# The norms between the stages of a two-block transformer pair: which instructions stand in their chain, and TensorE products repeated in their wait

## The chip, the cores and the metric

One Trainium2 chip, one of its cores. The time is device microseconds of one execution; lower is better. TensorE is called PE, VectorE DVE, ScalarE ACT, GpSimd POOL and SyncE SP.

## The reference

x is 256 tokens of 1024 values in float32. It goes through two blocks of a first kind, and then through two blocks of a second kind. A block of the first kind ends both of its halves with a layer norm of the residual, one of the second kind begins both of its halves with an rms norm:

```python
for l in range(DEPTH):                      # first kind, DEPTH = 2
    y = hybrid_mixer(x, ...)
    x = layer_norm(DN_ALPHA * x + y, ln1_g[l], ln1_b[l])
    y = conv_gated_ffn(x, ...)
    x = layer_norm(DN_ALPHA * x + y, ln2_g[l], ln2_b[l])
...
y = rmsnorm(x, g)                           # second kind: norm_mix, and norm_ffn alike
    # = x * rsqrt(mean(x * x) + NORM_EPS) * g
x = x + branch(y)
```

## The kernel before, in words

Everything runs as one long stream of weight products. A weight is cut into "halves" of 128 x 1024 values, 602 in all. Each half is loaded into `raw`, copied by ACT to a rounded high part `hi` (line 344), and POOL subtracts the two to get the low part `lo` (line 353). PE then makes three products for each tile (lines 146 to 148: high by high, low by high, high by low). There are four buffers of halves (`HALVES`), so the copy of half h waits for the products of half h - 4. `Stream.act`, `.pool`, `.dve` and `.pe` issue this stream on each engine up to a position; `end()` of a stage is 2 x (its last half + 1). `main.act(act, self.end())` therefore includes the copy of the fourth half of the next stage, which waits for the very last product of this one.

Between two stages stands a norm, where PE has nothing to multiply. The 256 tokens are two tiles of 128 tokens (tt = 0, 1), each in two column halves of 512. The last weight of a stage gives its sums in this order: tile 0 columns 0 to 511, tile 0 the rest, tile 1 the same, some 0.7 us apart. `Stream.by_tokens` changes that for the last four halves of the program: first all their products for tile 0, then all for tile 1.

- `Norm1` (`ln1` and `ln2` of the first kind, four times): DVE adds the residual (line 1046), takes statistics (1048, 1050), ACT takes the root (1022), DVE the reciprocal (1054) and writes `xn` (1057). PE transposes `xn` in 16 pieces (1011), ACT applies gain and bias (1029), DVE splits the result into `x_hi` (1075) and `x_lo` (1077), pair by pair of the eight 128-row pieces, and PE starts on the next stage's products as the pairs come. POOL rebuilds the residual `x_tok` from `xn` (lines 1095 and 1096), a quarter in the wait and the others between the coming low parts.
- The last `Norm1` has no transposes. DVE alone makes its full result in `x_tok` (1057, 1065, 1066), and the first `Norm2` follows on that.
- `Norm2` (`norm_mix` and `norm_ffn`, four times): the same with DVE statistics (1182 to 1185), root 1156, reciprocal 1189, `xn` 1192, transposes 1145, `x_hi` on ACT 1163 and `x_lo` on DVE 1198.
- `Final`: squares and their sum on ACT (1230), in place of DVE statistics.

## Time and profile before

| | us |
|---|---|
| median of 3 runs | 2162.07 (2160.2 to 2164.91) |
| profiled execution, its own time | 2160.19 |
| its span | 2158.4 |
| PE busy | 2084.0 (97%) |
| ACT busy | 1059.7 (49%) |
| POOL busy | 1498.1 (69%) |
| mean granted clock of PE | 0.984 of full |

The table is read from the left: the span is what the profile covers, and the execution's own time is 1.8 us more. Busy times overlap. A granted clock of 1.0 is 2.4 GHz and 0.5 is 1.2 GHz.

### The profile page before, as it was taken

What the parts mean: (1) busy time and instruction counts of PE and PEld (TensorE: products, weight loads), DVE (VectorE), ACT (ScalarE), POOL (GpSimd) and SP (SyncE); (2) the same over time, 40 slices, a digit from 0 to 9 for tenths busy, and PEclk for the clock granted to TensorE, in tenths of its full rate; (3) what the DMA queues carried; (4) which work ended last, traced back from release to release, by engine and by line L of the source; (5) the groups of instructions that cost most, each with busy time, mean ns of one, the idle gap of its engine ahead of it and who ended that gap; (6) DMA issues with size and microseconds to landing.
All of it is one profiled execution on the core that took longest, in us unless ns stands there. A gap on an engine that the chain in (4) does not pass through costs nothing.

```text
span 2158.4 us, 38524 instructions
## 1 busy us (share of the span) xinstructions
PE 2084.0 (97%) x16616; PEld 1921.1 (89%) x16616; DVE 899.3 (42%) x1498; ACT 1059.7 (49%) x1500; POOL 1498.1 (69%) x632
## 2 busy tenths in 40 slices
PE   7989989999969999999999899999999999998998
PEld 6889978799959989899999899899898999998998
DVE  5353247465355547374113211355473651132112
ACT  5555554555546453256444444465532564444444
POOL 6679887689856535367778688765353677786886
PEclk9999999999989999999999999999999999999999
DMA  8436544435534323234445455533232444454553
GB/s 346 142 126 208 193 166 141 154 121 195 193 137 137 118 82 116 99 137 157 156 157 191 149 187 181 190 137 119 79 118 91 145 157 156 157 182 151 184 187 127
DMA packets 47193, 332.89 MB, mean 154 GB/s; under 512 B 5168, under 2 KB 5552, under 8 KB 7856
## 3 DMA queue, kind: packets, MB, share of 16 engines
q1 hardware_dynamic: 47024, 330.43, 44.2%
q8 instruction: 131, 2.15, 0.4%
q14 instruction: 38, 0.31, 0.0%
HBM read 329.36 MB, written 1.05 MB: 153 GB/s over the span
## 4 chain that ended last, share of the span: by engine, by line
PE 68%; DVE 2%; ACT 1%; issue 0%; POOL 0%; DVEq 0%; ACTq 0%
PE bank L146 16%; PE bank L147 15%; PE bank L148 15%; PE y L146 3%; PE y L148 3%; PE y L147 3%; PE bank L1816 1%; PE bank L1828 1%; PE bank L1826 1%; PE bank L1856 1%; PE bank L1873 1%; PE bank L1876 1%; PE bank L1657 1%; PE bank L1867 1%; DVE bn L1182 1%; PE bank L1757 0%
## 5 line engine op out<-in xcount | busy, mean ns | idle before, releaser
L353 POOL TENSOR_TENSOR w_lo<-w_raw,w_hi 128x1024 fp32r<-128x1024 f32 x602 | 1462.4, 2436 | 642.8 <-ACT w_hi L344 642.6
L344 ACT ACTIVATE w_hi<-w_raw 128x1024 fp32r<-128x1024 f32 x602 | 636.7, 1059 | 929.0 <-PE bank L148 759.3
L146 PE MATMUL bank<-x_hi,w_hi 128*128 128x256 f32 x2960 | 866.2, 293 | 18.0 <-POOL w_lo L353 13.3
L147 PE MATMUL bank<-x_lo,w_hi 128*128 128x256 f32 x2960 | 842.0, 284 | 0.0
L148 PE MATMUL bank<-x_hi,w_lo 128*128 128x256 f32 x2960 | 841.8, 284 | 0.0
L146 PEld LDWEIGHTS bank<-x_hi,w_hi 128*128 128x128 f32 x2960 | 572.0, 193 | 41.1 <-issue 19.1
L147 PEld LDWEIGHTS bank<-x_lo,w_hi 128*128 128x128 f32 x2960 | 572.7, 193 | 6.7 <-issue 4.8
L148 PEld LDWEIGHTS bank<-x_hi,w_lo 128*128 128x128 f32 x2960 | 572.0, 193 | 0.0
L881 DVE SCALAR_TENSOR_TENSOR conv<-bank,par_sb,conv 128x254 f32<-128x254 f32 (+1 forms) x176 | 76.8, 478 | 213.7 <-ACT conv L869 212.1
L1298 DVE TENSOR_TENSOR hid_lo<-hid,hid_hi 128x512 fp32r<-128x512 f32 x22 | 45.1, 2048 | 241.2 <-ACT hid_hi L1293 241.2
L146 PE MATMUL y<-w_hi,hid_hi 128*128 128x512 f32 x352 | 139.9, 397 | 3.7 <-DVE hid_lo L903 3.7
L148 PE MATMUL y<-w_hi,hid_lo 128*128 128x512 f32 x352 | 139.0, 395 | 0.0
L147 PE MATMUL y<-w_lo,hid_hi 128*128 128x512 f32 x352 | 139.0, 395 | 0.0
L146 PEld LDWEIGHTS y<-w_hi,hid_hi 128*128 128x128 f32 x352 | 66.3, 188 | 19.7 <-DVE hid_lo L903 5.8
L148 PEld LDWEIGHTS y<-w_hi,hid_lo 128*128 128x128 f32 x352 | 66.2, 188 | 15.8
L1436 DVE SCALAR_TENSOR_TENSOR conv<-bank,par_sb,conv 128x255 f32<-128x255 f32 (+1 forms) x144 | 62.5, 477 | 41.3 <-ACT conv L1427 39.6
L147 PEld LDWEIGHTS y<-w_lo,hid_hi 128*128 128x128 f32 x352 | 66.2, 188 | 13.8
L1560 DVE SCALAR_TENSOR_TENSOR gate<-gate,bank 128x512 f32<-128x512 f32 x16 | 11.0, 688 | 130.5 <-PE bank L148 130.5
L146 PE MATMUL bank<-w_hi,x_hi 128*128 128x512 f32 x128 | 53.3, 416 | 0.0
L147 PE MATMUL bank<-w_lo,x_hi 128*128 128x512 f32 x128 | 50.0, 391 | 0.0
L148 PE MATMUL bank<-w_hi,x_lo 128*128 128x512 f32 x128 | 50.0, 391 | 0.0
L869 ACT ACTIVATE conv<-bank,par_sb 128x256 f32<-128x256 f32 x88 | 44.1, 551 | 0.0
(394 smaller groups left out, 3003.2 us busy)
## 6 DMA issues: line engine op xcount, KB each, us to landing
w_raw<-w SPq DMA_DIRECT2D x300, 1024.0 KB, 4.8
ln_rows<-ln_rows SPq DMA_DIRECT2D x4, 1024.0 KB, 7.7
mem_tok<-mem SPq DMA_DIRECT2D x2, 1024.0 KB, 4.9
const_sb<-const SPq DMA_DIRECT2D x1, 1536.0 KB, 8.2
par_sb<-par SPq DMA_DIRECT2D x2, 553.5 KB, 10.8
xn<-xT SPq DMA_DIRECT2D x1, 1024.0 KB, 4.9
w_raw<-w SPq DMA_DIRECT2D x2, 512.0 KB, 5.0
x_tok<-x SPq DMA_DIRECT2D x1, 1024.0 KB, 6.9
```

The costliest lines, as they stand in the source:

```text
L146: pe.matmul(out, lhs[0], rhs[0], start=start, stop=False, skip_group_check=skip)
L147: pe.matmul(out, lhs[0], rhs[1], start=False, stop=False, skip_group_check=skip)
L148: return pe.matmul(out, lhs[1], rhs[0], start=False, stop=stop, skip_group_check=skip)
L344: act.activation(self.hi[:, h % HALVES, :], self.raw[:, n % RAWS, i * HW:(i + 1) * HW], ACT.Copy).then_inc(*sig.up("high", h))
L353: pool.tensor_tensor(self.lo[:, h % HALVES, :], self.raw[:, n % RAWS, i * HW:(i + 1) * HW], self.hi[:, h % HALVES, :].bitcast(F32), ALU.su ...
L869: ins = act.activation(cb[:, j, :], view[:, j, :], ACT.Identity, scale=taps[:, 2, c0 + j:c0 + j + 1], bias=bias[:, c0 + j:c0 + j + 1])
L881: ins = dve.scalar_tensor_tensor(cb[:, j, tap:T], view[:, j, 0:T - tap], taps[:, 2 - tap, c0 + j:c0 + j + 1], cb[:, j, tap:T], ALU.mult, A ...
L1182: ins = dve.bn_stats(net.bn[:, tt, half, :], net.xtok[:, tt, c])
L1298: dve.tensor_tensor(net.hs2[1][:, 2 * (i % 3):2 * (i % 3) + 2, :], m["hid"][:, i % 2, :, :], net.hs2[0][:, 2 * (i % 3):2 * (i % 3) + 2, :] ...
L1436: ins = dve.scalar_tensor_tensor(cb[:, j, tap:T], two(b)[:, j, 0:T - tap], taps[:, 3 - tap, c0 + j:c0 + j + 1], cb[:, j, tap:T], ALU.mult, ...
L1657: pe.matmul(bank[b][:, :], K("ones"), m["keys"][:, j, :, :].rearrange("p i t -> p (i t)"), start=True, stop=True).then_inc(*sig.up("key_su ...
L1816: mm = pe.matmul(yd[g][r, (n % 4) * CH:(n % 4 + 1) * CH], h["mt"][r, n, :], h["t"][r, n, :], start=True, stop=True)
```

## The change

It touches the seven places between stages, and nothing inside them:

1. **Norm1** (three places). ACT gets its root table before the last two weight copies, and the fourth copy of the next stage moves behind the norm. ACT writes `xn` of tile 0; DVE only that of tile 1. POOL's first rebuild of `x_tok` waits until all of `xn` is there. PE repeats 14 products of the old `x_hi` behind the stage's last one, and 7 more behind tile 0's transposes.
2. **Norm2** (three places). Table load and fourth copy move alike. ACT squares and sums `x_tok` in place of DVE's statistics, and writes the last quarter of `xn`. PE repeats 12 products.
3. **Border** (a new class; it replaces the last `Norm1` and the first `Norm2`). The last four halves of `w_down` are ordered by tokens, so that tile 0 is normalised during tile 1's products; for this the last three down units stand at the stage's end. A norm's four DVE passes of 128 x 512 over a tile take the place of six. Transposes and splits go by tile. PE repeats 52 products, and 10 small ones of the identity between the tiles.

```diff
-    def by_tokens(self, first):
-        group = range(first, first + HALVES)
-        self.parts[2 * first:2 * (first + HALVES)] = [(h, part) for part in range(2) for h in group]
+    def by_tokens(self, last):
+        first = last + 1 - HALVES
+        group = range(first, last + 1)
+        self.parts[2 * first:2 * (last + 1)] = [(h, part) for part in range(2) for h in group]
...
@@ Feed1.__init__
-            if i:
+            if 0 < i < (11 if l < DEPTH - 1 else 9):
                 self.units.append(self.add_down(i - 1))
-        self.units.append(self.add_down(10))
+        for i in ((10,) if l < DEPTH - 1 else (8, 9, 10)):
+            self.units.append(self.add_down(i))
...
@@ Norm1.pe
         net.main.pe(pe, self.end())
+        net.repeat(pe, self.tb[3], 14)
         for tt in range(TT):
+            if tt:
+                net.repeat(pe, net.bank[4], 7)
...
@@ Norm1.act
-        net.main.act(act, self.end())
+        net.main.act(act, self.end() - 6)
+        act.preload_act_table_set("sqrt_and_others")
+        net.main.act(act, self.end() - 2)
...
+            if tt == 0:
+                act.wait_ge(*sig.at("inverse", *k_l))
+                act.wait_ge(*sig.at("product", self.after().last))
+                for half in range(2):
+                    c = slice(half * HALF, (half + 1) * HALF)
+                    act.activation(net.xn[:, 0, c], net.xtok[:, 0, c], ACT.Identity, scale=net.rs[:, 0:1], bias=net.ms[:, 0:1]
+                                   ).then_inc(*sig.up("xn_act", *k_l, half))
...
+        net.main.act(act, self.end())
@@ Norm1.dve, the new order
+        residual(0, 0)
+        statistics(0, 0)
+        residual(0, 1)
+        statistics(0, 1)
+        variance(0)
+        residual(1, 0)
+        inverse(0)
+        dve.scalar_tensor_tensor(net.ms[:, 0:1], net.mv[:, 0, 0:1], -1.0, net.rs[:, 0:1], ALU.mult, ALU.mult
+                                 ).then_inc(*sig.up("inverse", *k_l))
+        statistics(1, 0)
+        residual(1, 1)
+        statistics(1, 1)
+        variance(1)
+        inverse(1)
...
@@ Norm1.pool
         net.main.pool(pool, self.end())
...
+        pool.wait_ge(*sig.at("xn_act", *k_l, 1))
+        pool.wait_ge(*sig.at("xn", *k_l, 1))
...
@@ Norm2.pe and Norm2.act
+        net.repeat(pe, self.tb[3], 12)
...
+            act.wait_ge(*sig.at("x_new", *k_l, tt, 1))
+            act.activation(net.xn2[:, tt, :], net.xtok[:, tt, :], ACT.Square, accum_out=net.ms[:, tt:tt + 1]
+                           ).then_inc(*sig.up("x_squared", *k_l, tt))
...
+        act.wait_ge(*sig.at("inverse", *k_l))
+        act.activation(net.xn2[:, 1, HALF:D], net.xtok[:, 1, HALF:D], ACT.Copy, scale=net.rs[:, 1:2]).then_inc(*sig.up("xn_act", *k_l))
...
@@ Border.pe
+        net.main.pe(pe, self.end())
+        net.repeat(pe, self.tb[0][3], 52)
+        for tt in range(TT):
+            if tt:
+                pe.wait_ge(*sig.at("var", *self.first, 1))
+                for _ in range(10):
+                    pe.matmul(self.tb[1][3][:, 0:P], net.K("ident"), net.K("ident"), start=True, stop=True)
...
@@ Border.act
+        main.act(act, self.end() - 6)
+        act.preload_act_table_set("sqrt_and_others")
+        root_first(0)
+        act.wait_ge(*sig.at("x_new", *self.second, 0, 0))
+        main.act(act, self.end() - 4)
+        squares(0)
+        root(0)
+        root_first(1)
...
+        main.act(act, self.end())
...
@@ Net
+    def repeat(self, pe, bank, times):
+        for _ in range(times):
+            pe.matmul(bank[:, 0:T], self.xs[0][:, 0, 0:P], self.xs[0][:, 0, :], start=True, stop=True)
```

Three places show what moves. In the names, `w_hi` is a weight copy, `sd` the root, `xn` and `xn_189` the normalised tokens and `x_sb`, `x_hi` the transposed ones; numbers behind a name are buffers.

ACT at `ln1` of the first block, before:

```order
L344 ACTIVATE w_hi<-w_raw 128x1024 x3
L1022 ACT_TABLE_LOAD
L1022 ACTIVATE sd_60<-mv,const_sb 128x1 x2
L1029 ACTIVATE x_sb<-bank,par_sb 128x256 x8
L344 ACTIVATE w_hi<-w_raw 128x1024 x2
```

and after:

```order
L1022 ACT_TABLE_LOAD
L345 ACTIVATE w_hi<-w_raw 128x1024 x2
L1027 ACTIVATE sd_60<-mv,const_sb 128x1
L1033 ACTIVATE xn<-x_tok,ms_59,rs_61 128x512 x2
L1027 ACTIVATE sd_60<-mv,const_sb 128x1
L1039 ACTIVATE x_sb<-bank,par_sb 128x256 x8
L345 ACTIVATE w_hi<-w_raw 128x1024 x3
```

The table load stands two copies earlier, one of the copies has gone behind the eight `x_sb` steps, and two `xn` steps are new between the roots.

ACT at the border, from the last `hid_hi` on, before:

```order
L861 ACTIVATE hid_hi<-hid 128x512
L344 ACTIVATE w_hi<-w_raw 128x1024 x4
L1022 ACT_TABLE_LOAD
L1022 ACTIVATE sd_60<-mv,const_sb 128x1 x2
L1156 ACTIVATE sd_60<-ms_59,const_sb 128x1 x2
L1163 ACTIVATE x_hi<-bank,par_sb 128x256 x8
L344 ACTIVATE w_hi<-w_raw 128x1024 x2
```

and after, where line 1265 is the layer norm's root, 1272 a square, 1277 the rms norm's root, 1299 `xn` and 1284 `x_hi`:

```order
L861 ACTIVATE hid_hi<-hid 128x512
L345 ACTIVATE w_hi<-w_raw 128x1024 x3
L1289 ACT_TABLE_LOAD
L1265 ACTIVATE sd_60<-mv,const_sb 128x1
L345 ACTIVATE w_hi<-w_raw 128x1024
L1272 ACTIVATE xn_189,bn<-x_tok 128x512 x2
L1277 ACTIVATE ms_59<-ms_59,const_sb 128x1
L1265 ACTIVATE sd_60<-mv,const_sb 128x1
L1299 ACTIVATE xn_189<-x_tok,rs_61 128x512 x2
L1284 ACTIVATE x_hi<-bank,par_sb 128x128 x4
L1272 ACTIVATE xn_189,bn<-x_tok 128x512 x2
L1277 ACTIVATE ms_59<-ms_59,const_sb 128x1
```

Three copies instead of four stand ahead of the load, a fourth ahead of the squares, and the squares and `xn` steps are ACT's now.

DVE at the border, before, from the last statistics of the layer norm on:

```order
L1048 BN_STATS bn<-x_tok 128x6
L1050 BN_AGGR mv<-bn 128x2
L1054 RECIPROCAL rs_61<-sd_60 128x1
L1057 TENSOR_SCALAR xn<-x_tok,mv,rs_61 128x512
L1065 TENSOR_TENSOR x_tok<-xn,ln_rows 128x512
L1066 TENSOR_TENSOR x_tok<-x_tok,ln_rows 128x512
L1057 TENSOR_SCALAR xn<-x_tok,mv,rs_61 128x512
L1065 TENSOR_TENSOR x_tok<-xn,ln_rows 128x512
L1066 TENSOR_TENSOR x_tok<-x_tok,ln_rows 128x512
L1054 RECIPROCAL rs_61<-sd_60 128x1
```

and after, from its first variance on (1336 subtracts the mean and multiplies by the gain, 1343 multiplies by the reciprocal and adds the bias):

```order
L1328 BN_AGGR mv<-bn 128x2
L1336 SCALAR_TENSOR_TENSOR x_tok<-x_tok,mv,ln_rows 128x512 x2
L1340 RECIPROCAL rs_61<-sd_60 128x1
L1343 SCALAR_TENSOR_TENSOR x_tok<-x_tok,rs_61,ln_rows 128x512 x2
L1323 SCALAR_TENSOR_TENSOR x_tok<-x_tok,y 128x512
L1325 BN_STATS bn<-x_tok 128x6
L1348 TENSOR_TENSOR ms_59<-bn 128x1
L1323 SCALAR_TENSOR_TENSOR x_tok<-x_tok,y 128x512
L1325 BN_STATS bn<-x_tok 128x6
L1328 BN_AGGR mv<-bn 128x2
L1353 RECIPROCAL rs_61<-ms_59 128x1
L1336 SCALAR_TENSOR_TENSOR x_tok<-x_tok,mv,ln_rows 128x512 x2
```

Tile 0's layer norm now stands ahead of tile 1's residual, and each tile's passes are four instead of six.

## Rows read from the trace of the kernel before

**Rows 1.** The page: span, PE busy and its granted clock in 40 slices
```profile
span 2158.4 us, 38524 instructions
...
PE   7989989999969999999999899999999999998998
...
PEclk9999999999989999999999999999999999999999
```

**Rows 2.** Waits of PE over the span: total us, times, longest us
```profile
PE bank L1145 <- DVE xn L1192: 30.9, 4, 16.0
PE bank L1011 <- DVE xn L1057: 14.6, 7, 4.5
PE bank L146 <- POOL w_lo L353: 13.3, 3, 11.4
```

**Rows 3.** Windows: stretch, its length, each engine's busy us and starts, granted clock, DMA
```profile
110.60:120.39 9.79, 4.05 (x19) 2.45 (x17) 9.09 (x17) 5.28 (x10) 6.36 (x4) 0.78 0.54 202
120.39:126.30 5.91, 5.91 (x28) 5.91 (x29) 2.94 (x6) 1.76 (x5) 0.00 (x0) 0.50 0.00 0
...
323.36:327.70 4.34, 4.34 (x20) 4.34 (x21) 2.94 (x6) 1.41 (x4) 0.00 (x0) 0.50 0.01 4
...
433.36:437.00 3.64, 3.64 (x17) 3.64 (x18) 2.94 (x6) 1.40 (x4) 0.00 (x0) 0.51 0.00 0
626.00:646.77 20.77, 3.71 (x19) 3.10 (x17) 17.90 (x39) 5.41 (x12) 4.20 (x2) 0.67 0.30 101
646.77:652.70 5.93, 5.93 (x48) 5.91 (x49) 2.54 (x8) 2.20 (x5) 1.45 (x1) 1.00 0.00 0
1196.15:1205.84 9.69, 4.02 (x18) 3.30 (x17) 7.40 (x19) 4.82 (x10) 3.58 (x2) 0.82 0.55 201
1205.84:1211.80 5.96, 5.96 (x49) 5.93 (x50) 2.21 (x6) 2.20 (x5) 1.48 (x1) 1.00 0.01 3
...
1962.51:1966.10 3.59, 3.59 (x17) 3.59 (x18) 2.20 (x6) 1.13 (x4) 0.00 (x0) 0.50 0.02 5
```

**Rows 4.** Timeline of DVE, norm ln1 of the first block: start, us, [idle before]
```profile
108.96 0.69 DVE L1046 SCALAR_TENSOR_TENSOR x_tok<-x_tok,y 128x512 f32<-128x512 f32 x1 [5.58 <-PE y L148]
...
114.85 1.00 DVE L1057 TENSOR_SCALAR xn<-x_tok,mv,rs 128x512 f32<-128x512 f32 x2
...
115.96 2.70 DVE L1057 TENSOR_SCALAR xn<-x_tok,mv,rs 128x512 f32<-128x512 f32 x2
...
119.55 0.69 DVE L1077 TENSOR_TENSOR x_lo<-x_sb,x_hi 128x512 fp32r<-128x512 f32 x1
```

**Rows 5.** Timeline of ACT and POOL in the same norm
```profile
112.17 1.28 ACT L1022 ACT_TABLE_LOAD   x1
...
115.54 1.43 POOL L1095 TENSOR_TENSOR x_tok<-xn,ln_rows 128x512 f32<-128x512 f32 x1 [0.96 <-DVE xn L1057]
```

**Rows 6.** Timeline of DVE and ACT, norm_ffn of the first block
```profile
1194.49 0.69 DVE L1180 TENSOR_TENSOR x_tok<-x_tok,y 128x512 f32<-128x512 f32 x1 [13.17 <-PE y L148]
...
1201.96 0.89 DVE L1192 TENSOR_SCALAR xn<-x_tok,rs 128x512 f32<-128x512 f32 x2
...
1203.95 2.67 ACT L1163 ACTIVATE x_hi<-bank,par_sb 128x256 fp32r<-128x256 f32 x7 [2.75 <-PE bank L1145]
```

**Rows 7.** Timeline of DVE and ACT in the last norm
```profile
2146.07 1.39 DVE L1249 TENSOR_TENSOR x_tok<-x_tok,y 128x512 f32<-128x512 f32 x2 [6.30 <-PE y L148]
...
2151.65 1.38 DVE L1249 TENSOR_TENSOR x_tok<-x_tok,y 128x512 f32<-128x512 f32 x2 [1.27 <-PE y L148]
...
2146.79 0.63 ACT L1230 ACTIVATE xn<-x_tok 128x512 f32<-128x512 f32 x1 [3.18 <-DVE x_tok L1249]
```

**Rows 8.** Timeline of POOL in the products behind ln1
```profile
139.74 1.62 POOL L1096 TENSOR_TENSOR x_tok<-x_tok,ln_rows 128x512 f32<-128x512 f32 x1
141.32 9.95 POOL L353 TENSOR_TENSOR w_lo<-w_raw,w_hi 128x1024 fp32r<-128x1024 f32 x4
```

**Rows 9.** One line of DVE: count, shortest/median/longest ns, first and last start
```profile
L1298 DVE TENSOR_TENSOR hid_lo<-hid,hid_hi x22: 1996/2006/2480, 1225.7 to 2137.3; 128x512 fp32r<-128x512 f32 x22
```

More of the change, by code:

```diff
@@ L922, in last_low @@
             state_low(dve, 10)
-        self.units[-3].dve = last_low
+        last.dve = last_low
     def add_down(self, i):
@@ L1105, in sp @@
                          ).then_inc(*sig.up("pos_loaded", by=16))
-        net.main.send(sp, net.main.halves[self.after().last][0] + 1 + (5 if self.last else 12 if self.key == "ln1" else 9))
+        net.main.send(sp, net.main.halves[self.after().last][0] + 1 + (12 if self.key == "ln1" else 9))
         if self.l == 0:
@@ L1126, with __init__ @@
 class Norm2:
[L1129 removed]
+    def __init__(self, net, key, l, after, more):
         self.net, self.key, self.l, self.after, self.more = net, key, l, after, more
@@ L1182, in dve @@
-                ins = dve.bn_stats(net.bn[:, tt, half, :], net.xtok[:, tt, c])
-            step(ins)
-            step(dve.bn_aggr(net.mv[:, tt, :], net.bn[:, tt, :, :]))
-            dve.scalar_tensor_tensor(net.ms[:, tt:tt + 1], net.mv[:, tt, 0:1], net.mv[:, tt, 0:1], net.mv[:, tt, 1:2],
-                                     ALU.mult, ALU.add).then_inc(*sig.up("var", *k_l, tt))
+                if tt == TT - 1 and half == 1:
+                    dve.wait_ge(*sig.at("product", self.after().last))
+                else:
+                    dve.wait_ge(*sig.at("summed", self.more, tt, half))
@@ L2048, in act @@
         self.weighted_high(act, 5)
-        main.act(act, 2 * (self.units[-1].last + 1))
+        main.act(act, 2 * (self.units[-1].last + 1) - 2 * HALVES)
     def chain_act(self, act, hf, key_log):
@@ L2482, in __init__ @@
         self.main = Stream(sig, raw, hi, lo, units)
-        self.main.by_tokens(len(self.main.halves) - HALVES)
+        for s in self.stages:
+            if isinstance(s, (Border, Final)):
+                self.main.by_tokens(s.after().last)
     def K(self, name):
```

260 lines of the change are left out of this document (183 added, 77 removed).

## The prediction

> **What bounds the kernel now.** I read the page first [rows 1]. PE is busy in nine tenths or more of nearly every slice, and its granted clock is full outside a few slices. So the products set the time, and only the places where PE has none can be shortened. The list of PE's waits names them [rows 2]: transposes behind `xn`, 30.9 us for four `Norm2` (16.0 of it at the border) and 14.6 us for three `Norm1`. The 13.3 us behind POOL are 11.4 us at the start of the program, which the change doesn't touch.
>
> The windows put a length on each place, from the start of a stage's last product to the first product of the next [rows 3]: 9.79 us at `Norm1` (three such places, alike within 0.04 us), 9.69 us at `Norm2` (three, alike within 0.01), 20.77 us at the border. They also show a second cost. The clock falls to 0.5 in each wait, and in four of seven places the next stage's products begin at it: for 5.91, 4.34, 3.64 and 3.59 us. At 0.5 half of such time is lost, 8.7 us in all. Behind the border and behind `norm_ffn` of the first block the clock was back at 1.00 when the products began.
>
> **Norm2, three places.** Before, the first residual starts at 1194.49, `xn` of tile 1 at 1201.96, `x_hi` at 1203.95 and the first product at 1205.84 [rows 3, 6]. After, DVE only adds: tile 0 is whole 1.4 us after 1194.49, at 1195.9, and tile 1's last half, which waits for the last product, at 1197.3. A square of 512 columns takes ACT 0.63 us [rows 7]; for 1024 I take 1.1, and 0.2 for reading the sum, 0.3 for the root. That gives tile 0's root at 1197.5 and tile 1's at 1199.0. Reciprocal and half an `xn` (0.89 / 2) end at 1199.6. The last quarter of `xn` is ACT's, beside it. Two transposes at the full clock and their latency bring `x_hi` to 1200.05 instead of 1203.95. Behind it nothing changes, so each place saves 3.9 us, **11.6 us** for three. The bounds: 3.0 if the square costs 0.4 more for each tile, 4.3 if the tiles overlap better. The 12 repeats cost nothing: 48 starts in 5.93 us are 0.12 us each [rows 3], 1.5 us behind a last product at 1196.4, and tile 0's `xn` isn't there before 1198.1.
>
> **Norm1, three places.** Here DVE keeps the statistics. Its tile 0 `xn` goes to ACT (1.00 us of DVE less [rows 4]), one reciprocal and a one-column product (0.4) go ahead of tile 1's statistics, and tile 1's root is no longer covered (0.4). So tile 1's `xn` starts at 115.7 instead of 115.96. What matters more is its length: before, both halves took 2.70 us beside POOL's `x_tok`, against 1.00 us for the pair ahead of it [rows 4, 5]. POOL now waits. The first half is ready 1.0 us earlier, and transposes at the full clock give 0.3: 1.3 us a place, **3.9 us**. The fillers (1.7 us, then 0.8) end before the `xn` they might hold up, at 112.7 against 113.6, and at 115.4 against 116.3.
>
> The Trainium skill (GPSIMD Engine Reference, Specifications) says that POOL shares its SBUF interfaces with DVE instructions of two SBUF inputs or in a two-port mode; by that rule the four passes of the border are exposed too, and the next part takes it up with a row.
>
> **The table load.** Its 1.28 us ends at 113.45 [rows 5], ahead of DVE's need for the first root, so its move is worth nothing by itself; it only makes the earlier reciprocal possible. The Trainium skill (ScalarE: Activation LUTs, What ACT_TABLE_LOAD costs) adds a drain and comes to 2.66 us for a switch: by that the root would have come at 114.8, some 0.2 us late in each `Norm1`, and the sum would grow by 0.6 us.
>
> **The border.** Let T be the end of tile 0's products. Tile 1's take 5.6 us more (2151.65 less 2146.07 in the last norm, which has that order [rows 7]). DVE's residual and statistics of tile 0 end at T + 2.3. The table load stands behind a copy that waits for a quarter of those 5.6 us, T + 1.5; with 1.1 for the copy, 1.3 for the load and 0.3 for the root, that is there at T + 4.3. The two passes before it and the two behind have two SBUF inputs, and POOL's low part runs from T + 2.7. Such an instruction that starts under a low part takes 2.00 us [rows 9] instead of 0.69 [rows 4]. I let one of the four pay that: tile 0's new x is there at T + 7.5, when tile 1's products are over too. From there: squares to T + 9.6; tile 1's residual and statistics to T + 11.3; `xn` of tile 0 on ACT to T + 12.9; tile 1's four passes to T + 14.5; its squares, root and reciprocal to T + 16.4; `xn` half 0.5, transposes, and x_hi; DVE still has two pairs of tile 0's `x_lo` in front of tile 1's first, so the first product starts at T + 19.1. From the last product's start (T + 5.2) that is 13.9 us against 20.77: **6.9 us**. Bounds: 5 if two more passes meet a low part, 8.5 if none does. The 52 repeats run until T + 11.8, 0.4 us short of tile 0's `xn`. The three down units at the stage's end give their `hid_lo` more cover; that is worth 0.5 us of a small wait which I don't rest on.
>
> **Clock.** If it stayed full, the four stretches would come back: 1.8 us at `norm_ffn` of the last block, but only 1.5, 0.8 and 0.5 us behind `Norm1`, because there the first products then wait for `x_lo`, about 1.0 us a pair (2.94 us for six instructions [rows 3]) where six products take 0.72: **4.6 us**. Does it stay? With the fillers no gap without PE work is as long as before: 0.5, 0.6 and 1.4 us at `Norm2`, 1.0, 0.9 and 1.8 us at `Norm1`; but at the border 2.5 us remain before tile 1's transposes and 1.5 behind them. I take it that `Norm2` mostly holds the clock (0.5 us lost in all), `Norm1` often doesn't (2.1 us of it lost), and the border loses it for some 4 us of products, where before none was: 2.0 us lost.
>
> **POOL behind Norm1.** The fourth low part (2.4 us) and the first quarter of `x_tok` (2.9 us) used to lie in the wait and now lie in the stage. Four low parts took 9.95 us and a quarter's second half 1.62 us [rows 8], so four halves and a quarter are 12.9 us of POOL against 11.6 us of PE (24 x 0.12 each). POOL's lead is used up near the third and fourth quarter. I take 0.5 us; up to 2 us for each `ln1`.
>
> **Sum.** 11.6 + 3.9 + 6.9 + 0.5 + 4.6 - 0.5 - 2.1 - 2.0 - 0.5 = 22.4. From the profiled 2160.19 that is 2137.8; I say 2138, which is 24 us under the median of 2162.07. A change under 0.2% (4.3 us) can't be told from none here.
>
> **Rivals.**
> - The sum as it stands, 2133 to 2143: 0.57.
> - The clock holds everywhere: 4.6 us come in again, and more at the border: 2131. For it: every gap shrinks. Against: the border. 0.12.
> - The fillers don't hold the clock. Every place then loses about 4.4 us of products at half speed, 2.2 us x 7 = 15.4 against 8.7 before: 22.9 - 6.7 = 16.2, so 2144. The Trainium skill (TensorE: Matmul & The Clock Gate, A second HAM failure mode) tells of a kernel whose short idle pieces between groups brought the slow clock back again and again, which speaks against such a patchwork. 0.17.
> - POOL becomes the bound behind all three `Norm1` and its low parts delay PE by 2 to 3 us each: 2145. For it: [rows 8]. 0.09.
> - ACT's chain replaces DVE's one for one, and neither norm is shorter: 2158. Against: a square beside a residual is two engines at work. 0.03.
> - Slower: the clock falls during the fillers and stays down over the first products. It was down for 10.2 us in all at `ln1` (9.79 x 0.22 x 2, and 5.91 [rows 3]); if all of that lay on products, seven places would lose 36 us, 27 more than now, and the 52 repeats would take 12.5 us and end 6 us late. 22.9 gained, 33 lost: 2171. It decides from about 7 us of half speed on products in each place. 0.02.
>
> **How the numbers follow.** The likeliest case gives 2138, 2133 to 2143 by its own bounds. The range of 8 in 10 takes in both clock cases in part, 2130 to 2147. Faster holds for all but the last two: 0.95; within 0.2% 0.03; slower 0.02.
>
> **What the profile after would show.** First products at 5.8 us behind the last at `Norm2`, 8.5 at `Norm1`, 14 at the border; `xn` of line 1057's successor at 0.55 us for each half in `Norm1`; a granted clock of 1.00 behind `Norm2` and about 0.7 in the 6 us behind the border; POOL's low parts just in time near the third quarter of `x_tok`. I am wrong if the transposes wait for fillers, if more of the border's DVE passes take 2 us, or if the clock behind `Norm2` reads 0.5.

## The result, and the profile after

The changed kernel took 2148.01 us (median of 4 runs, 2147.72 to 2149.55); the kernel before took 2163.21 beside it (4 runs, 2160.20 to 2164.91). The ratio is 0.9932 with a 95% interval of 0.9916 to 0.9948: 15 us less, where 24 had been forecast (2138, with a range of 2130 to 2147). The direction was right, and the time lies 1 us above the range.

The profiled execution took 2147.97 us. The page, with the rows that answer to [rows 1]:

```profile
span 2146.2 us, 38890 instructions
...
PE   7999999999999999999999999999999999999998
...
PEclk9999999999999999999999999999999999999999
```

PE is now busy for nine tenths or more of every slice but the first and the last, and the granted clock is nine tenths or more in all of them. Part of that busy time is repeats. PE's waits over the span (total us, times, longest us), beside [rows 2]:

```profile
PE bank L146 <- POOL w_lo L354: 16.3, 5, 11.2
PE bank L146 <- DVE x_lo L1095: 5.1, 3, 1.7
PE bank L146 <- DVE x_lo L1220: 3.8, 3, 1.3
PE bank L1014 <- ACT xn L1033: 3.8, 3, 1.3
PE s L519 <- DVE aqk L754: 3.0, 1, 3.0
```

Of the 30.9 and 14.6 us behind `xn`, 9.1 are left, over several rows; the repeats fill a part of the wait. Two rows are worse outside the norms: the wait behind POOL's low parts grew from 13.3 us in three places to 16.3 in five, and a wait of 3.0 us on `aqk` has appeared, in the middle of a mixer. (The waits on `x_lo` grew too, from 1.7 to 5.1 us behind `Norm1` and from 3.1 to 3.8 behind `Norm2`; they are the last stretch of the norm's own chain, and the windows below hold them.) The windows that answer to [rows 3], from a stage's last product to the first product of the next, and behind it:

```profile
111.61:120.38 8.77, 5.30 (x40) 4.37 (x38) 6.90 (x16) 4.47 (x10) 1.26 (x1) 1.00 0.26 104
120.38:126.30 5.92, 5.89 (x34) 5.57 (x35) 2.94 (x6) 3.20 (x6) 3.50 (x2) 0.71 0.00 0
312.97:321.71 8.74, 5.32 (x40) 4.38 (x38) 6.87 (x16) 4.47 (x10) 1.92 (x1) 1.00 0.47 178
427.70:436.66 8.96, 5.30 (x39) 4.36 (x38) 6.90 (x16) 4.46 (x10) 1.27 (x1) 1.00 0.25 103
630.70:645.10 14.40, 11.21 (x90) 10.37 (x89) 13.29 (x31) 9.36 (x29) 2.69 (x2) 1.00 0.21 74
645.10:651.10 6.00, 6.00 (x50) 6.00 (x51) 1.74 (x8) 3.57 (x6) 4.36 (x2) 1.00 0.00 0
1197.10:1202.88 5.78, 4.00 (x31) 3.31 (x29) 3.84 (x10) 5.19 (x13) 1.27 (x1) 1.00 0.41 160
1202.88:1208.90 6.02, 6.02 (x49) 6.00 (x50) 2.20 (x6) 3.14 (x6) 3.86 (x2) 1.00 0.14 20
```

`Norm2` went from 9.69 to 5.78 us, `Norm1` from 9.79 to 8.77, 8.74 and 8.96, the border from 20.77 to 14.40. That alone is 21 us. So where did the rest go? For each weight half I took the moment at which PE begins its products in either trace, and the difference of the two. The difference grows where the change gains and shrinks where it loses, and it ends at 12.2 us. (Before's profiled execution lay 3 us under its median, so the traces show 12.2 where the medians show 15.2. Part of this can be seen: in it the clock was back at 1.00 when the products behind the border began, while in the traces of the experiments `e2`, `e3` and `e16` below, which have the same old border, 3.6 to 4.9 us of these products ran at 0.5.) Its steps:

| place | step, us | forecast |
|---|---|---|
| three `Norm2` | +11.7 (3.91 each) | +11.6 |
| three `Norm1` | +2.8 (1.01, 1.01, 0.82) | +3.9 |
| border with the three down units ahead | +5.5 | +6.9 + 0.5 |
| clock in the products behind the norms | +2.8 | 0.0 (4.6 - 0.5 - 2.1 - 2.0) |
| second mixer of the first kind, halves 104 to 107 | -5.7 | not in the sum |
| products behind `ln1` of the second block | -1.1 | -0.5, for all POOL |
| start of `Mixer2` behind the border | -1.3 | not in the sum |
| two falls of the clock in mid product | -2.6 | not in the sum |

The second mixer is the largest loss. DVE and POOL there, first in the kernel before, then in the changed one (start, us):

```profile
364.22 1.50 DVE L753 TENSOR_TENSOR aqk<-aqk,const_sb 128x512 f32<-128x512 f32 x1
365.75 2.77 DVE L754 TENSOR_TENSOR aqk<-aqk,rope 128x512 f32<-128x512 f32 x1
...
369.38 0.69 DVE L805 TENSOR_TENSOR cu<-cu,sq 128x512 f32<-128x512 f32 x1
...
370.59 2.30 DVE L753 TENSOR_TENSOR aqk<-aqk,const_sb 128x512 f32<-128x512 f32 x1
372.92 0.69 DVE L754 TENSOR_TENSOR aqk<-aqk,rope 128x512 f32<-128x512 f32 x1
...
369.69 2.65 POOL L353 TENSOR_TENSOR w_lo<-w_raw,w_hi 128x1024 fp32r<-128x1024 f32 x1 [1.72 <-ACT w_hi L344]
```

```profile
362.35 2.77 DVE L753 TENSOR_TENSOR aqk<-aqk,const_sb 128x512 f32<-128x512 f32 x1
365.16 2.77 DVE L754 TENSOR_TENSOR aqk<-aqk,rope 128x512 f32<-128x512 f32 x1
...
368.79 2.31 DVE L805 TENSOR_TENSOR cu<-cu,sq 128x512 f32<-128x512 f32 x1
...
371.62 0.68 DVE L753 TENSOR_TENSOR aqk<-aqk,const_sb 128x512 f32<-128x512 f32 x1
372.33 2.72 DVE L754 TENSOR_TENSOR aqk<-aqk,rope 128x512 f32<-128x512 f32 x1
...
368.14 2.40 POOL L354 TENSOR_TENSOR w_lo<-w_raw,w_hi 128x1024 fp32r<-128x1024 f32 x1 [0.77 <-ACT w_hi L345]
371.88 2.62 POOL L354 TENSOR_TENSOR w_lo<-w_raw,w_hi 128x1024 fp32r<-128x1024 f32 x1 [1.33 <-ACT w_hi L345]
```

The passes of lines 753 and 754 stand there twice; they are the rope passes of the queries and then of the keys. A DVE pass of two SBUF operands that starts under a low part waits the low part out: the one of 368.79 ends 0.56 us behind its low part (370.54), the one of 372.33 ends 0.55 behind its own (374.50), and alone such a pass takes 0.69. The rows show five passes in a chain, and a low part lengthens three of them before (1.50, 2.77, 2.30) and four now (2.77, 2.77, 2.31, 2.72), among them the last, for which PE's attention scores wait. Over 0.69 us each that is 4.5 us before and 7.8 now; the chain starts 0.3 us earlier against PE, so it ends 3.0 us later, and that is PE's wait. PE starts nothing from 371.79 to 375.10, and then its clock is down, which makes up the rest of the 5.7 us (windows as above, first of the changed kernel, then of the one before):

```profile
374.40:381.40 7.00, 6.24 (x26) 5.39 (x28) 2.86 (x6) 0.85 (x1) 0.10 (x1) 0.51 0.43 152
```

```profile
374.40:381.40 7.00, 6.97 (x51) 6.26 (x52) 5.29 (x10) 4.40 (x11) 3.83 (x2) 1.00 0.43 150
```

26 starts against 51 in the same 7 us. DVE and POOL in the border of the changed kernel show the same thing three times:

```profile
627.98 3.55 DVE L1336 SCALAR_TENSOR_TENSOR x_tok<-x_tok,mv,ln_rows 128x512 f32<-128x512 f32 x2
...
634.94 1.19 DVE L1348 TENSOR_TENSOR ms<-bn 128x1 f32<-128x1 f32 x1 [0.43 <-ACT xn L1272]
...
637.81 1.40 DVE L1336 SCALAR_TENSOR_TENSOR x_tok<-x_tok,mv,ln_rows 128x512 f32<-128x512 f32 x2
...
654.10 2.38 DVE L2344 TENSOR_SCALAR ab<-y 8x256 f32<-8x256 f32 x1
...
628.13 2.85 POOL L354 TENSOR_TENSOR w_lo<-w_raw,w_hi 128x1024 fp32r<-128x1024 f32 x1 [4.36 <-ACT w_hi L345]
633.69 2.42 POOL L354 TENSOR_TENSOR w_lo<-w_raw,w_hi 128x1024 fp32r<-128x1024 f32 x1 [2.71 <-ACT w_hi L345]
646.74 9.59 POOL L354 TENSOR_TENSOR w_lo<-w_raw,w_hi 128x1024 fp32r<-128x1024 f32 x4 [10.63 <-ACT w_hi L345]
```

Line 1336 takes 3.55 us for tile 0 and 1.40 for tile 1; a sum of one column takes 1.19; and behind the border a product of 8 x 256 elements takes 2.38, until 0.15 us behind the last of four low parts; in `e4_border_only` below it takes 0.28.

**The theory.** The change moved weight copies, and with them POOL's low parts, onto DVE passes for which PE waits. By it, that cost 5.7 us in the mixer, about 1.3 behind the border, some 2 in it, and 1.1 as lateness of POOL itself. The rivals: the losses are of the clock and of chance; or they come from PE's products arriving at another time, with the long passes only going along.

### The profile page after: what moved, and what is told of

Its sections match the earlier page's. It is cut to its first block, busy times and chain, and to the rows that moved or that the text cites. A ratio compares the mean times of both kernels' runs of the same rounds, so it can differ in the third digit from the quotient of the medians.

```text
span 2146.2 us, 38890 instructions
## 1 busy us (share of the span) xinstructions
PE 2096.5 (98%) x16787; PEld 1933.0 (90%) x16787; DVE 876.6 (41%) x1464; ACT 1078.2 (50%) x1539; POOL 1501.0 (70%) x632
## 4 chain that ended last, share of the span: by engine, by line
PE 67%; DVE 2%; ACT 1%; POOL 0%; issue 0%; DVEq 0%; ACTq 0%
PE bank L146 17%; PE bank L147 15%; PE bank L148 15%; PE y L146 3%; PE y L148 3%; PE y L147 2%; PE bank L2001 1%; PE bank L2013 1%; PE bank L2011 1%; PE bank L2041 1%; PE bank L2058 1%; PE bank L2061 1%; PE bank L1842 1%; PE bank L2052 1%; PE bank L1942 0%; POOL w_lo L354 0%
## 5 line engine op out<-in xcount | busy, mean ns | idle before, releaser
L146 PE MATMUL bank<-x_hi,w_hi 128*128 128x256 f32 x2960 | 866.1, 293 | 26.5 <-POOL w_lo L354 16.3
```

Source lines behind the costliest of these rows:

```text
L146: pe.matmul(out, lhs[0], rhs[0], start=start, stop=False, skip_group_check=skip)
```

## The experiments

Each was timed in five rounds beside the kernel before, whose median was 2163.85 us beside the first four, 2162.29 beside e5 to e8, 2162.38 beside e9 to e12 and 2162.08 beside e13 to e16. It moved by up to 1.8 us between these groups, so a difference of a few tenths to about 2 us between two medians is not shown by itself, above all where the kernels are of different groups. Where the text rests on less, it takes the step in the traces (the same differences of PE's products as above), and each trace is one execution.

### Which part gave what: e1 to e4

`e1_norepeat` is the changed kernel without the repeats:

```diff
-        for _ in range(times):
+        for _ in range(0):
             pe.matmul(bank[:, 0:T], self.xs[0][:, 0, 0:P], self.xs[0][:, 0, :], start=True, stop=True)
```

and the same for the ten products of the identity in the border. The other three put the norms of before back (`OldNorm1`, `OldNorm2`) in all places but one kind. Of `e3_norm1_only`:

```diff
-            self.stages += [feed, Norm1(self, "ln2", l, self.y, before) if l < DEPTH - 1 else Border(self, before)]
+            self.stages += [feed, Norm1(self, "ln2", l, self.y, before) if l < DEPTH - 1 else OldNorm1(self, "ln2", l, self.y, before, True)]
...
-                self.stages.append(Norm2(self, "norm_mix", l, before, ("fout", l - 1)))
+                self.stages.append(OldNorm2(self, "norm_mix", l, before, ("fout", l - 1)))
```

> The changed kernel without any repeated product (52, 14 + 7, 12 and the 10 of the identity). If the repeats are what keeps the clock at 1.00, the chains stay as short as in the changed kernel (8.5 us at Norm2, 8.8 at Norm1, 19 at the border), the clock falls to 0.5 in most waits, and the time is 5 to 9 us above the changed kernel: 2153 to 2157. If the shorter waits alone keep it, or if the repeats themselves delay the transposes, it is within 1 us of the changed kernel or below it.

> Only the three Norm2 of the change; Norm1 and the border as before. My account of the two traces: three times 3.9 us, and 1 to 2 us of clock: 13 to 14 us below before, 2149 to 2150, which is nearly all of what the whole change brought. The rival, that the parts help each other through the clock, gives less than 11 us.

> Only the three Norm1 of the change. Theory one: the postponed low part and quarters of x_tok put POOL's work beside DVE's rotary passes of the second mixer, which costs 5.7 us there, and makes POOL late behind the third Norm1 (1 us); with 1.0 us of chain and up to 1 us of clock at each of three places the sum is 1 to 4 us slower than before. Rival: the wait in the mixer comes from something else in the changed kernel, and Norm1 alone is 3 to 5 us faster than before.

> Only the border of the change, with the down units at the stage's end. By the two traces: 5.6 us gained up to the second product half of the next stage, 1.3 us given back two halves later, where PE then waits longer for POOL: 4 to 5 us below before. Rival: the give-back belongs to the clock or to Norm1's delays, and the border alone brings 5.5 us or more.

| kernel | median us (runs) | ratio to before, 95% |
|---|---|---|
| `e1_norepeat` | 2148.63 (5) | 0.9933, 0.9920 to 0.9947 |
| `e2_norm2_only` | 2152.39 (5) | 0.9948, 0.9936 to 0.9961 |
| `e3_norm1_only` | 2163.93 (11) | 1.0002, 0.9994 to 1.0011 |
| `e4_border_only` | 2156.73 (5) | 0.9967, 0.9955 to 0.9980 |

`Norm2` alone gives 11.5 us by the medians, 3.91 us in each of its three places in the trace, less than the 13 to 14 expected, since the clock added little. The border alone gives 7.1 by the medians, more than the 4 to 5 expected and within what the rival said (5.5 or more). Its trace lies only 3.9 us ahead of before's, which is itself 3.7 under the median of its group: it holds the 5.5 us of the table above and another 1.5 of clock behind the last `norm_ffn`, and against them 1.4 behind the border, where the clock is at 0.5 from 642.0 to 645.4, just behind the first product at 641.54, and 1.4 of clock behind a `Norm2`. The 1.3 us two halves behind the border, which the expectation put down to the border, are not lost in it. So that loss needs the other parts of the change. `Norm1` alone gives nothing, between the two theories: its three gains are all there (1.0, 1.0 and 0.8), and so is a loss of 5.5 us in the second mixer and the 1.1 us behind `ln1`. Neither e2 nor e4 has the mixer's loss. So that loss belongs to the new `Norm1`, as both theories allow; the rival of e3's expectation, that it comes from something else in the changed kernel, is out.

By the medians the repeats are worth 0.6 us, which can't be told from none (the ratios are 0.9933 and 0.9932). That is the second case of the expectation; in the first it would have been 5 to 9. (The 8.5 and 19 us for `Norm2` and the border in that expectation are not the lengths of the windows above, 5.78 and 14.40.) The clock in e1 is down for 63 us in all against 30 in the changed kernel, but mostly while PE has nothing to do or waits for `x_lo`; behind all three `Norm2` it is full without a single repeat.

### Putting the weight copy back: e5 to e7

`e5_early_copy` is the changed kernel with two edits in `Norm1`: the fourth weight copy ahead of tile 0's `xn` on ACT, and POOL's first quarter of `x_tok` behind the last `x_lo`.

```diff
             if tt == 0:
+                net.main.act(act, self.end())
                 act.wait_ge(*sig.at("inverse", *k_l))
...
             ins.then_inc(*sig.up("xt", *k_l, i))
-        net.main.act(act, self.end())
...
-        pool.wait_ge(*sig.at("xn_act", *k_l, 1))
-        pool.wait_ge(*sig.at("xn", *k_l, 1))
+        pool.wait_ge(*sig.at("x_low", *k_l, 3))
```

> The changed kernel with two edits in Norm1: ACT makes the fourth weight copy between tile 0's root and tile 0's xn (in the wait, as before the change), and POOL's first quarter of x_tok waits for the last x_lo instead of for tile 1's xn. Theory one (the postponed fourth low part pushes POOL's low parts onto passes of DVE for which PE waits, 5.66 us in the second mixer of the first kind and 1.1 us behind ln1 of the second block): both losses go, 6 to 7 us, so 2141 to 2143; the low part then runs from about 114.5 to 116.9 in the first ln1, just ahead of tile 1's xn, and the first product behind Norm1 stays within 0.3 us of where it is. Rival (the stall in the mixer comes from the products' own pace and the clock, which falls there by chance): no change, 2147 to 2149.

It measured 2143.34 us (4 runs, ratio 0.9910, 0.9896 to 0.9923), 4.7 less than the changed kernel and 0.3 above the expected range. In its trace the step in halves 104 to 107 is +5.8 us against the changed kernel, and the 1.1 us behind `ln1` are back too. The passes of the mixer in e5:

```profile
360.64 1.61 DVE L753 TENSOR_TENSOR aqk<-aqk,const_sb 128x512 f32<-128x512 f32 x1
...
363.83 1.96 DVE L805 TENSOR_TENSOR cu<-cu,sq 128x512 f32<-128x512 f32 x1
...
366.70 2.68 DVE L753 TENSOR_TENSOR aqk<-aqk,const_sb 128x512 f32<-128x512 f32 x1
```

So e5 is not free of overlaps. But line 754 takes 0.69 us both times, the low parts add 4.2 us to the chain in place of 7.8, and PE doesn't wait for it.

`e6_early_copy_only` has the first edit and not the second.

> As e5_early_copy, but POOL's first quarter of x_tok keeps its place right behind tile 1's xn, about 118.0 in the first ln1, where DVE makes the x_lo that the first product waits for (119.5). Theory one: that first subtraction of two SBUF operands waits for POOL's instruction, 0.7 becomes 1.2 to 2 us, and the first product of each of the three Norm1 comes 0.5 to 1.3 us later than in e5_early_copy, so 1.5 to 4 us above it: 2143 to 2146. Rival (the subtraction is not held up, since only whole blocks of POOL work matter): equal to e5_early_copy within 0.5 us.

2149.16 us (5 runs, ratio 0.9933, 0.9921 to 0.9945), 5.8 above e5. POOL's quarter now ran while DVE made the first `x_lo`. DVE's and POOL's rows at `ln1` of the first block in e6:

```profile
118.80 1.32 POOL L1113 TENSOR_TENSOR x_tok<-x_tok,ln_rows 128x512 f32<-128x512 f32 x1
...
119.04 1.63 DVE L1095 TENSOR_TENSOR x_lo<-x_sb,x_hi 128x512 fp32r<-128x512 f32 x1
```

and DVE's in e5:

```profile
118.88 0.69 DVE L1095 TENSOR_TENSOR x_lo<-x_sb,x_hi 128x512 fp32r<-128x512 f32 x1
```

PE's first product comes 1.10 us later in each of the three `Norm1`, and the wait on `aqk` in the mixer is back with 3.0 us. The price of a collision was forecast well. That the mixer's loss (4.5 us against e5) would return with it was not, and the total lies 3 us above the expected range: the copy alone doesn't cure it.

`e7_quarters_apart` changes one number of the changed kernel, the distance of the quarters behind `ln2`.

```diff
-                net.main.pool(pool, self.end() + 2 * (4 if self.key == "ln1" else 2) * (2 * tt + half))
+                net.main.pool(pool, self.end() + 2 * (4 if self.key == "ln1" else 3) * (2 * tt + half))
```

> The changed kernel with one number changed: behind ln2 the quarters of x_tok on POOL stand three weight halves apart instead of two, so POOL does the same work at other times. Theory one (it is where POOL's low parts lie under DVE's passes that decides, not how much POOL does): the 5.66 us stall in the second mixer of the first kind, halves 104 to 107, changes by more than 2 us, in whichever direction, and with it the total; most likely smaller, 2142 to 2146. Rival (POOL is simply short of time there): the stall stays at 5.5 to 6 us and the total at 2147 to 2149.

2149.32 us (5 runs, ratio 0.9934, 0.9921 to 0.9948). No gain; the loss in halves 104 to 107 became 1.1 us smaller, and 0.9 us went just ahead of it. The total is near what the rival said (2147 to 2149) though its stall, 4.6 us, is under the 5.5 to 6 of the rival, and it is a miss for me: moving the quarters does not by itself take the low part off the last rope pass, which again took 2.72 us.

### The border: e8

```diff
-        main.act(act, self.end() - 6)
+        main.act(act, self.end() - 8)
         act.preload_act_table_set("sqrt_and_others")
         root_first(0)
         act.wait_ge(*sig.at("x_new", *self.second, 0, 0))
-        main.act(act, self.end() - 4)
+        main.act(act, self.end() - 6)
         squares(0)
         root(0)
+        main.act(act, self.end() - 4)
```

and in `root`, in place of DVE's sum:

```diff
-            act.activation(net.ms[:, tt:tt + 1], net.ms[:, tt:tt + 1], ACT.Sqrt, scale=1.0 / D, bias=net.K("eps")
+            act.activation(net.ms[:, tt:tt + 1], net.bn[:, tt, 0, 0:1], ACT.Identity, scale=1.0 / D, bias=net.K("eps")
...
+            act.activation(net.ms[:, tt:tt + 1], net.bn[:, tt, 1, 0:1], ACT.Sqrt, scale=1.0 / D, bias=net.ms[:, tt:tt + 1]
```

> The changed kernel with the border's ACT order changed: the first weight copy waits for tile 0's new x as the second did, the second comes behind tile 0's root, and the sum of the two half squares is made on ACT (a scaled copy, then the root with it as bias) instead of by DVE. So no low part of POOL lies under the first two passes of line 1336, nor under the sum. Theory one (the two passes took 3.55 us instead of 1.40, the sum 1.19 instead of 0.16, because of the low parts): tile 0's new x comes 2.1 us earlier and the root some 1 us more; the first product behind the border comes 2 to 3 us earlier, so 2145 to 2146.5, if no low part meets another pass. Rival (tile 1's residual and statistics set the end of the border, and tile 0 has slack): 0 to 0.5 us earlier, 2147.5 to 2149.

2146.20 us (5 runs, 2144.62 to 2151.01, ratio 0.9929, 0.9916 to 0.9941); that spread doesn't show a gain over the changed kernel by itself. In the trace the border's step is 1.66 us, less than the 2 to 3 forecast. DVE and POOL of e8 say why:

```profile
626.39 1.41 DVE L1341 SCALAR_TENSOR_TENSOR x_tok<-x_tok,mv,ln_rows 128x512 f32<-128x512 f32 x2
...
632.58 3.55 DVE L1341 SCALAR_TENSOR_TENSOR x_tok<-x_tok,mv,ln_rows 128x512 f32<-128x512 f32 x2
...
632.65 2.93 POOL L354 TENSOR_TENSOR w_lo<-w_raw,w_hi 128x1024 fp32r<-128x1024 f32 x1 [0.27 <-ACT w_hi L345]
```

The pass of tile 0 shrank from 3.55 to 1.41 us as forecast, and the same pass of tile 1 grew from 1.40 to 3.55, because the second low part had moved onto it.

### Together, and with less or more filling: e9 to e12

`e9_both_moves` has the edits of e5 and of e8.

> The edits of e5_early_copy (Norm1's fourth weight copy early, the first quarter of x_tok behind the last x_lo) and of e8_border_copies (the border's weight copies moved, the sum of squares on ACT) together. Theory one (both only move POOL's low parts off passes of DVE, at different places): the gains add, 4.7 from the one and 1.7 from the other, so 2141 to 2142.5. Rival (the border's gain is only passed on to a later wait when the stages ahead of it stand at another phase): 2143 to 2144, as e5_early_copy alone.

2140.85 us (4 runs, 2139.00 to 2143.30, ratio 0.9903, 0.9888 to 0.9918). That is slightly below the expected 2141 to 2142.5; the gains add, within what the spread allows.

`e10_abs_on_act`, on top of e9:

```diff
-        step(dve.tensor_scalar(ab, y, -1.0, None, ALU.mult))
-        dve.tensor_tensor(ab, y, ab, ALU.max).then_inc(*sig.up("absed2", l))
...
-        act.wait_ge(*sig.at("absed2", l))
+        act.activation(m["ab2"][:, :], m["small"][:, 1, :], ACT.Abs, bias=net.prm2(l, "dt_bias")[0:8, :]
+                       ).then_inc(*sig.up("y_size", l))
+        act.wait_ge(*sig.at("y_size", l))
```

> e9_both_moves, and ACT makes the absolute value that the first decay row of Mixer2 starts from (one ACTIVATE) in place of DVE's two small instructions, the first of which took 2.38 us instead of 0.28 behind the border, since a low part of POOL ran. Theory one (that wait is what makes ACT's copies late and PE's gap at the third to fourth unit 2.49 us instead of 1.24): 0.5 to 1.3 us less than e9_both_moves, unless the next small instruction of DVE waits in its place. Rival (the gap has another cause): equal within 0.3 us.

2139.20 us (4 runs, 2138.26 to 2140.04, ratio 0.9896, 0.9879 to 0.9913), 1.65 less, with runs that overlap those of e9. PE's gap ahead of half 192, from one start to the next, went from 2.48 us in e9 to 0.94.

`e11_no_fillers` is e9 with the edit of e1.

> e9_both_moves without any repeated product (52, 14 and 7, 12, and the 10 with the identity). Theory one (what the full clock gives behind the norms is small, since the first products there wait for x_lo anyway): 0.5 to 2.5 us above e9_both_moves. Rival (the fillers were worth little in the changed kernel only because the mixer's stall hid it): 3 to 6 us above.

2142.60 us (4 runs, 2141.91 to 2143.35, ratio 0.9911, 0.9896 to 0.9925): 1.75 above e9, whose slowest run is as slow as these. All repeats together are worth between nothing and 1.8 us.

`e12_more_fillers` is e9 with, behind the last transposes of each `Norm1`:

```diff
+        for _ in range(7):
+            pe.matmul(net.bank[4][:, 0:P], net.K("ident"), net.K("ident"), start=True, stop=True)
```

> e9_both_moves with seven products of the identity more, behind the last transposes of each Norm1, where PE has nothing for 2.0 us before the first product (e5_early_copy: the clock fell there at 321.8 and at 431.0). They take about 1.7 us. Theory one (the fall there comes from that last empty stretch): the clock stays full over the first products of all three Norm1 and the time falls by 0.5 to 1.5 us. Rival (the fall comes from the stretches before, or the first product is held up by them): no change, or up to 0.5 us slower.

2142.40 us (4 runs, 2141.85 to 2144.10, ratio 0.9911, 0.9896 to 0.9926), 1.55 above e9 by the medians. Both theories missed. The clock did what theory one said. The window behind `ln2` of the first block, first of e12, then of e5, which has the same `Norm1` without these products:

```profile
320.00:326.00 6.00, 5.80 (x34) 4.82 (x35) 3.39 (x8) 2.58 (x5) 2.88 (x3) 1.00 0.00 0
```

```profile
319.99:326.00 6.01, 5.94 (x29) 5.26 (x30) 2.94 (x6) 2.35 (x5) 2.56 (x2) 0.72 0.00 0
```

PE gained 2.5 us on e9 between halves 93 and 100: 1.0 where the window lies, and 1.5 some 20 us later, where e9's clock falls in mid product (343.7 us) and e12's doesn't. Then it lost 0.9 and, in halves 104 to 107, 4.4 us: with PE and DVE earlier, the low parts lay on both passes again. DVE in e12:

```profile
365.21 2.31 DVE L805 TENSOR_TENSOR cu<-cu,sq 128x512 f32<-128x512 f32 x1
...
368.76 2.72 DVE L754 TENSOR_TENSOR aqk<-aqk,rope 128x512 f32<-128x512 f32 x1
```

### Taking only the overlap away: e13 to e16

What e7 and e12 had left open is whether the overlap causes the loss or only goes with a certain timing. `e13_low_held` is the changed kernel with one wait more:

```diff
+        if l == 1:
+            main.pool(pool, self.at(10))
+            pool.wait_ge(*sig.at("roped", l, 1))
         main.pool(pool, self.at(27))
```

> The changed kernel with one wait more: in the second mixer of the first kind POOL begins the low parts of halves 108 and later only when DVE's last rope pass has ended (they are needed 12 to 15 us later, so PE doesn't wait for them). Nothing else moves. Theory one (the overlap of low parts with the product of line 805 and the pass of line 754 is the cause): these two take 0.69 us each instead of 2.31 and 2.72, PE's scores come some 3 us earlier, the clock stays up behind them, and the 5.66 us come back nearly whole: 2142.5 to 2144. Rival (the phase of PE against ACT causes it, and the long passes only go with it): 2147 to 2149.

2141.85 us (4 runs, ratio 0.9907, 0.9894 to 0.9921), 6.2 less than the changed kernel, and 0.65 below the expected range. The same rows of DVE, three lines further down in this kernel, and POOL's:

```profile
365.77 0.69 DVE L808 TENSOR_TENSOR cu<-cu,sq 128x512 f32<-128x512 f32 x1
...
367.85 0.69 DVE L757 TENSOR_TENSOR aqk<-aqk,rope 128x512 f32<-128x512 f32 x1
...
368.62 9.43 POOL L354 TENSOR_TENSOR w_lo<-w_raw,w_hi 128x1024 fp32r<-128x1024 f32 x4 [4.26 <-DVE aqk L757]
```

Both passes take 0.69 us, the wait on `aqk` is gone from PE's list, and the step in halves 104 to 107 is 5.8 us. POOL does the same work, only later; its low parts then lie on DVE passes behind the scores (line 739 takes 2.04 us, line 814 2.70), and PE waits for none of them.

The 18 traces agree. In the seven with the mixer's loss (the changed kernel, e1, e3, e6, e7, e8, e12: 4.4 to 5.7 us) the last rope pass takes 2.71 or 2.72 us, and low parts add 5.8 us or more to the five passes. In the other eleven that pass takes 0.69 and the addition is 4.9 us or less.

> e10_abs_on_act with the seven products of the identity behind the last transposes of each Norm1 (as e12_more_fillers) and the wait of e13_low_held. Theory one (e12's gain of 2.4 us of clock at ln2 was eaten by 4.4 us in the mixer, which the held low part takes away): 1 to 3 us less than e10_abs_on_act, 2136.5 to 2138.5. Rival (bringing PE ahead there is given back at the next wait anyway): 2139 to 2140.

> e10_abs_on_act with the wait of e13_low_held and nothing else. There the mixer shows no loss, so by theory one the control changes little: between 0 and 2 us less (one rope pass of 2.68 us still met a low part in e5_early_copy). Rival (holding POOL back costs, since its low parts pile up behind): up to 1 us more.

> The kernel before the change with the same wait. In its trace the pass of line 753 took 2.30 us instead of 0.69 under a low part, and PE waited little. Theory one: 0 to 1.6 us less than before. Rival: no change or slower.

`e14_held_and_fillers`: 2137.26 us (4 runs, 2137.08 to 2137.98, ratio 0.9884, 0.9871 to 0.9898). `e15_held_best`: 2138.24 (4 runs, 2135.77 to 2140.07, ratio 0.9887, 0.9874 to 0.9901). `e16_before_held`: 2161.47 (11 runs, ratio 0.9993, 0.9984 to 1.0002). The fillers that cost 1.55 us in e12 cost nothing once the low parts are held, and in the traces e14 keeps its lead of 1.3 us over e10 through the mixer. e14, e15 and e16 all came out within what theory one said for them. The difference of e14 to e15, 1.0 us, is within the spread of e15's runs, so it is not shown that the fillers pay. e16 comes out 0.6 us below before, which can't be told from none. e14 beats both kernels: 24.8 us under before beside it, a ratio of 0.9884, while the changed kernel's is 0.9932.

## Why the prediction was right and wrong

The sum said 22.4 us, and the forecast of 2138 took it off the profiled execution of 2160.19, which lay 1.9 us under the median of then and 3.0 under that of the measurement. From the medians the same sum gives 2139.7 and 2140.8. That much of the miss is the starting point. The rest is in the terms.

**Norm2: right.** The sum said 3.9 us for each place and a first product 5.8 us behind the last; the trace shows 3.91 and 5.78, three times, and `e2_norm2_only` shows it by itself.

**Norm1: right in kind, too large.** 1.3 us a place was forecast, 1.01, 1.01 and 0.82 came. Tile 0's `xn` on ACT and tile 1's on DVE in the changed kernel:

```profile
114.05 1.52 ACT L1033 ACTIVATE xn<-x_tok,ms,rs 128x512 f32<-128x512 f32 x2 [0.65 <-DVE ms L1078]
...
116.95 1.00 DVE L1087 TENSOR_SCALAR xn<-x_tok,mv,rs 128x512 f32<-128x512 f32 x2
```

The pair of tile 1 takes 1.00 us instead of 2.70 [rows 4], as forecast. But it starts at 116.95, 1.0 us after 115.96; this execution stood 1.0 us later by then (a fall of the clock at its start), so relative to the stage it starts at the old time, where 115.7 had been forecast, 0.26 earlier. So the steps moved ahead of tile 1's took what was to be gained: from the first residual to tile 1's `xn` it is 6.99 us now (109.96 to 116.95) and was 7.00 before (108.96 to 115.96).

**The border: one collision counted, two found in it.** I let one of four passes meet a low part for 1.3 us. The passes of line 1336 lost 2.1, the sum of squares lost 1.0, and I had not counted that sum as exposed at all. ("If more of the border's DVE passes take 2 us" was one of the three signs of being wrong, and the only one that came.) e8 took both losses away, and gained 1.66 us since another pass met the next low part. The three down units at the stage's end, forecast at +0.5, cost 0.8 us in front of the border.

**The clock: term wrong in both directions.** 2.0 us were to be lost behind the border and 2.1 behind `Norm1`; the clock stayed full behind the border, behind every `Norm2`, and behind the last `Norm1`. That is 2.8 us better than forecast, and luck is in it: in the traces of e4 and e13, which have the same new border, and of e10, which has e8's, the clock was at 0.5 for 3.2 to 3.4 us at the first products behind it, much as the prediction said. And the repeats have less to do with the clock than I had thought. Without them the total is at most 1.8 us longer (e1, e11), and the clock is full behind three `Norm2` in e1's trace and behind two of three in e11's. There the shorter waits alone do it; at `Norm1` the repeats cut the time at 0.5 from 10.2 us a place to 3.4 or nothing.

**POOL: the step that failed.** "POOL's lead is used up near the third and fourth quarter. I take 0.5 us" asked only whether a low part would come too late for PE. It did behind `ln1`, for 1.1 us. What a low part does to DVE while it runs was in the prediction, but for the border only, because there I looked for it. The rival that gave POOL a part (0.09) had PE wait for low parts behind all three `Norm1`, and that is not what cost the time either. The postponed fourth copy and first quarter shift the low parts that follow, through 14 weight halves of the next stage, and in the second mixer they came to lie longer on the passes ahead of the scores. That is the 5.7 us: 3.0 of wait and the rest at the slow clock behind it. e13 shows the cause: with one wait of POOL more, and no other edit, both passes take 0.69 us and the loss is gone. Together with the 1.3 us behind the border (e10 took it away; it is not lost in e13 either, which doesn't touch that place, so it comes and goes with the phase as well) and the 1.1, POOL's term was 8 us instead of 0.5.

The prediction named a rule of the Trainium skill (GPSIMD Engine Reference, Specifications) and applied it to the border. Another page of the Trainium skill (SBUF — State Buffer, Who interferes with whom) is more exact. It says that a DVE instruction with two SBUF inputs contends with a GpSimd instruction that reads SBUF, and of DVE in a two-port mode that whoever issues first has the shared pair for the whole instruction while the other fully blocks. The traces show such blocking, for passes with two SBUF inputs too, and on both sides: a pass of 0.69 us took 2.31 and 2.72 under a low part, and one of 0.28 took 2.38, while a low part that came second took 2.85 instead of 2.40.

What is left of the difference I put down to chance: the two falls of the clock in mid product, 2.6 us in the profiled execution. Other traces have them or lack them at the same two places; what brings them is not shown.

By these numbers the forecast's 22.4 becomes 22.4 - 1.1 (`Norm1`) - 1.9 (border and down units) + 2.8 (clock) - 7.6 (POOL) - 2.6 (chance) = 12.0, against 12.2 in the traces.

**Open.** Which of the two postponements, the copy or the quarter of `x_tok`, does what in the mixer isn't separated: e6 shows that the copy alone doesn't cure it, and the quarter's edit alone was not tried. Why the last rope pass stayed clear of low parts in e5 and not in e6 is told by the rows (in e6 PE's first products came 1.1 us later in each `Norm1`), not derived. One of e6's five runs took 2144.76 us where the others took 2148.41 to 2150.12, so the loss may come and go between executions of one kernel; only one trace of each is kept.

## What to carry to other kernels

When a change delays work on POOL, look for the DVE passes that it will now lie on, through the whole stage that follows and not only where the change is; a pass on PE's critical path can cost the rest of POOL's instruction, whatever its own size (1.0 us for a sum of one column, 2.1 for 8 x 256 elements, 2.0 for 128 x 512). Add the losses up along the whole chain that PE waits for, since slack hides them until their sum is too large: in these traces 4.9 us were hidden and 5.8 were not. Where the background work has slack, make it wait for the end of the critical pass: one wait gave 6.2 us by the medians and 5.8 in the trace, and with it the extra products of e12 no longer cost anything. Filling a wait with repeated products keeps the granted clock up, but price it by a run without them: the clock is worth only what the first products behind the wait can use, here 0.6 to 1.0 us a place behind `Norm1`, where they wait for `x_lo`, and 1.5 behind the last `Norm2`.

## What the runs showed that I had not expected

The clock falls in mid product, with no wait ahead of it (the longest time between two of PE's starts in the 14 us ahead is 0.5 us). It does so at a few places of the program, and at each in some traces and not in others: near 33 us in 11 of the 18 traces, near 343 in 15, near 700 in 4, near 1450 in 12. Windows of the changed kernel, and one of e5 whose place is undisturbed in the changed kernel:

```profile
33.10:36.50 3.40, 3.40 (x19) 3.40 (x17) 3.37 (x4) 0.00 (x0) 3.40 (x2) 0.50 1.05 393
705.60:709.00 3.40, 3.40 (x18) 3.40 (x17) 1.54 (x3) 0.47 (x1) 3.26 (x2) 0.51 0.39 106
```

```profile
1448.20:1451.60 3.40, 3.40 (x18) 3.40 (x17) 1.69 (x3) 0.62 (x1) 3.40 (x2) 0.50 0.39 92
```

Each costs 1.1 to 1.5 us. Their number may explain much of the spread between executions of one kernel; the runs of e15, for one, go from 2135.77 us at a mean granted clock of 0.997 to 2140.07 at 0.994. And bringing PE forward can cost more than it gives: e12 gained 2.5 us on e9 by half 100 and had lost 5.2 by half 107, with no instruction of the mixer changed.
